# Two routing stages take over the first token turn and the first weight chunk of the expert stage behind them, and TensorE multiplies constants in them

## The reference

```
def first_block(...):            # after the mixer
    u = layer_norm(x) * (1.0 + sc_f) + sh_f
    ffn = hierarchical_moe(u, w_grp, b_grp, w_exp, b_exp, w_e_gate, w_e_up, w_e_down)
    x = layer_norm(DEEPNORM_ALPHA * x + (1.0 + gt_f) * ffn, ln2_g, ln2_b)

def moe_ffn(h, w_router, b_router, w_gu, b_gu, w_dn, b_dn):      # second block
    logits = (h @ w_router + b_router).astype(jnp.float32)
    top_logits, top_e = lax.top_k(logits, TOP_K)
    top_w = jax.nn.softmax(top_logits, axis=-1)
    ... tokens sorted by expert, each expert's list padded to blocks of 128 ...
    gu = xe @ w_gu[e] + b_gu[e]
    act = (x_lin + 1) * (x_glu * jax.nn.sigmoid(SWIGLU_ALPHA * x_glu))
    return act @ w_dn[e] + b_dn[e]
```

## Time and profile before

| | us |
|---|---|
| median of 3 runs | 2674.14 |
| lowest, highest | 2674.13, 2677.97 |
| the profiled execution, its own time | 2678.14 |
| its span, first to last instruction | 2676.4 |

### The profile page before, as it was taken

How to read it: one execution, slowest core, us unless ns; L and a number is a source line. 1 busy time by engine, 2 the same in 40 slices (tenths; PEclk the granted TensorE clock), 3 DMA queues, 4 the chain that set the end, 5 groups by cost and what they waited for, 6 DMA issues and landing times. The chain is left out here.

```text
span 2676.4 us, 38805 instructions
## 1 busy us (share of the span) xinstructions
PE 2453.7 (92%) x11850; PEld 2003.5 (75%) x11850; DVE 2141.3 (80%) x2397; ACT 1640.8 (61%) x1930; POOL 518.1 (19%) x357
## 2 busy tenths in 40 slices
PE   7987869999979998788969999999999999999994
PEld 6845657887768886777757888888888888888883
DVE  7887757999854327786558999999999999999995
ACT  3245546777744326564236777777777777777773
POOL 1214011222200003100021222222221222222220
PEclk9988869999989998899959999999999999999997
DMA  9873238999963410201258999999999999999995
GB/s 350 284 271 122 52 120 302 357 379 383 348 208 97 142 56 1 81 15 64 81 177 312 375 379 367 369 361 368 368 371 374 363 362 364 367 368 377 371 365 171
DMA packets 258910, 711.97 MB, mean 266 GB/s; under 512 B 41379, under 2 KB 74418, under 8 KB 256594
## 3 DMA queue, kind: packets, MB, share of 16 engines
q1 hardware_dynamic: 232626, 640.70, 64.4%
q0 software_dynamic: 22240, 59.80, 8.0%
q10 hardware_dynamic: 3968, 10.49, 1.0%
HBM read 691.95 MB, written 41.49 MB: 274 GB/s over the span
## 5 line engine op out<-in xcount | busy, mean ns | idle before, releaser
L52 PE MATMUL psum_all<-sb_ring_r,sb_arena_r 128*128 128x512 f32 (+1 forms) x2352 | 908.5, 386 | 0.0
L166 DVE TENSOR_TENSOR sb_ring_r<-sb_ring,sb_hi_ring_r 128x1024 fp32r<-128x1024 f32 (+1 forms) x489 | 657.9, 1395 | 136.2 <-ACT sb_hi_ring_r L157 130.4
L157 ACT ACTIVATE sb_arena_r<-sb_ring 128x1024 fp32r<-128x1024 f32 (+1 forms) x462 | 506.9, 1152 | 161.8 <-DMA sb_ring<-in_w_gu_dram 138.9
L166 DVE TENSOR_TENSOR sb_ring_r<-sb_ring,sb_arena_r 128x1024 fp32r<-128x1024 f32 (+1 forms) x462 | 593.6, 1342 | 10.2 <-ACT sb_arena_r L157 9.6
L157 ACT ACTIVATE sb_hi_ring_r<-sb_ring 128x1024 fp32r<-128x1024 f32 (+1 forms) x489 | 554.2, 1192 | 42.8 <-DMA sb_ring<-in_w_in_dram 17.9
L52 PEld LDWEIGHTS psum_all<-sb_ring_r,sb_arena_r 128*128 128x128 f32 x2352 | 447.4, 190 | 93.2
L51 PE MATMUL psum_all<-sb_hi_ring_r,sb_arena_r 128*128 128x512 f32 (+1 forms) x1304 | 497.2, 381 | 17.2 <-DVE sb_ring_r L166 5.2
L53 PE MATMUL psum_all<-sb_hi_ring_r,sb_arena_r 128*128 128x512 f32 (+1 forms) x1304 | 493.2, 378 | 0.0
L51 PE MATMUL psum_all<-sb_arena_r 128*128 128x512 f32 x1064 | 426.9, 401 | 2.9 <-DVE sb_arena_r L2467 2.9
L53 PE MATMUL psum_all<-sb_arena_r 128*128 128x512 f32 x1080 | 427.8, 396 | 0.0
L51 PEld LDWEIGHTS psum_all<-sb_hi_ring_r,sb_arena_r 128*128 128x128 f32 x1304 | 248.1, 190 | 70.3 <-issue 10.5
(11 more groups left out here) (494 smaller groups left out, 3193.3 us busy)
## 6 DMA issues: line engine op xcount, KB each, us to landing
sb_ring<-in_w_gu_dram SPq DMA_DIRECT2D x544, 512.0 KB, 6.3
sb_ring<-in_w_dn_dram SPq DMA_DIRECT2D x272, 512.0 KB, 8.5
sb_ring<-in_w_e_gate_dram SPq DMA_DIRECT2D x36, 1024.0 KB, 7.4
sb_ring<-in_w_e_up_dram SPq DMA_DIRECT2D x36, 1024.0 KB, 7.5
sb_ring<-in_w_e_down_dram SPq DMA_DIRECT2D x36, 1024.0 KB, 7.1
sb_ring<-in_w_in_dram SPq DMA_DIRECT2D x27, 1024.0 KB, 6.1
sb_arena<-in_w_ada_dram POOLq DMA_DIRECT2D x32, 512.0 KB, 5.9
sb_ring<-in_w_mod_dram SPq DMA_DIRECT2D x16, 1024.0 KB, 8.6
```

The source lines that it names most:

```text
L52: eng.matmul(out, a[0], b[1], start=False, stop=False)
L157: act.activation(s.hi[c % len(s.hi)], s.raw[c % len(s.raw)], ACT.Copy).then_inc(s.hi_made, 1)
L166: dve.tensor_tensor(s.lo[c % len(s.lo)], s.raw[c % len(s.raw)], s.hi[c % len(s.hi)].bitcast(F32), ALU.subtract).then_inc(s.lo_made, 1)
```

## The change

- In both routings TensorE starts with three 128x512 fp32 multiplications of constants (`keep_warm`), and does two more behind the turn of item 0. Nothing reads their results.
- The turn of item 0's rows, their high and low halves, and those of chunk 0 move from `experts` to the end of `route`, on the same engines. In `experts` VectorE raises the semaphores that these steps raised.
- SyncE no longer waits in `project_and_normalise` for the store of `xn` to land; it waits at the chunks in `route`, and so does GpSimd ahead of clearing `xg`, a clearing that stood first in its program.
- SyncE starts the second half of the chunks only when GpSimd has issued the gather of item 0 (`sent`).
- First block: the group choice takes one 64-element operation in place of nine small ones; the expert number is copied by VectorE, not ScalarE; the softmax weights are worked out behind the list; ScalarE's exponential stands ahead of the context squares.
- Second block: `first_rows` 0 and 1 stand behind the list's products, not ahead of them.

```
+def keep_warm(pe, k, bank, times):
+    for _ in range(times):
+        pe.matmul(k.psum[:, bank, :], k.ident[:], k.neg_sel[:, 0:4, :].rearrange("p h n -> p (h n)"), start=True, stop=True)
...
-            sp.wait_ge(s.stored, 16 * TT)
...
+            sp.wait_ge(R.x_stored, 16 * TT)
             for c, src in enumerate(first_chunks(m, e)):
+                if c == chunks_ahead(m) // 2:
+                    sp.wait_ge(s.sent, 1)
                 sp.dma_start(raw[c].rearrange("p (a b) -> p a b", a=src.shape[1]), src).then_inc(R.ahead_landed[c], 16)
...
             pool.indirect_dma_start(xg, None, m.x, bass.IndirectOffsetOnAxis(ap=R.ids[:, 0:1].bitcast(U32), axis=0),
                                     bounds_check=T - 1, oob_is_err=False).then_inc(R.gathered, 16)
+            pool.sem_inc(s.sent, 1)
 
         @block.tensor
         def _(pe):
+            keep_warm(pe, k, 0, 3)
             pe.wait_ge(s.halves, 2)
...
+            pe.wait_ge(s.list_read, 1)
+            pe.wait_ge(R.gathered, 16)
+            for kk in range(KD):
+                ins = pe.transpose(x_banks[:, kk * P:(kk + 1) * P], xg[:, kk * P:(kk + 1) * P], k.ident[:])
+            ins.then_inc(s.x_turned, 1)
+            keep_warm(pe, k, RANKS, 2)
...
+                act.wait_ge(R.ahead_landed[0], 16)
+                act.activation(hi, raw[0], ACT.Copy).then_inc(s.w_hi, 1)
+            act.wait_ge(s.x_turned, 1)
+            act.activation(x_hi, x_banks, ACT.Copy).then_inc(s.x_hi, 1)
...
-                for t in range(TT):
-                    ins = dve.tensor_tensor(four(scores)[:, t], four(logits[:, :, G:])[:, t], sel[:, t], ALU.mult)
-                link(ins)
...
+                link(dve.scalar_tensor_tensor(out=by_group(scores), in0=wide(g_other.rearrange("p t g -> p (t g)"), 2, E // G),
+                                              scalar=NEG, in1=by_group(logits), op0=ALU.mult, op1=ALU.add))
...
+            if biased:
+                weigh()
             dve.wait_ge(s.ready, 1)
             dve.wait_ge(s.ranked, 1)
...
+            if not biased:
+                dve.wait_ge(s.expert_row, 1)
+                dve.tensor_copy(R.expert_i[:, 0:NI], k.psum[:, ROW, 0:NI]).then_inc(s.items, 1)
...
+            def split_first():
+
+                dve.wait_ge(s.w_hi, 1)
+                dve.tensor_tensor(lo, raw[0], hi.bitcast(F32), ALU.subtract)
+
+            def split_rows():
+
+                dve.wait_ge(s.x_hi, 1)
+                dve.tensor_tensor(x_lo, x_banks, x_hi.bitcast(F32), ALU.subtract)
...
-            turn_x(0, True)
             pe.wait_ge(s.x_lo, 1)
...
-            make_hi(act, k, ss, 0)
             make_hi(act, k, ss, 1)
-            read_x(0, 0, False)
...
-            make_lo(dve, k, ss, 0)
-            lo_x(0, 0)
+            dve.sem_inc(ss.hi_made, 1)
+            dve.sem_inc(ss.lo_made, 1)
+            dve.sem_inc(s.x_turned, 1)
+            dve.sem_inc(s.x_hi, 1)
+            dve.sem_inc(s.x_lo, 1)
```

More of the change, by code:

```diff
@@ L1799, in route @@
     RANKS, TURNED, LIST, ROW = (4, 5, 6, 7) if biased else (1, None, 3, 2)
+    X_BANKS = slice(6, 8) if biased else slice(2, 4)
     BEYOND = T if biased else top * T
@@ L1841, in route @@
         assert at[0] <= FIRST_Y_AT - ROUTE_AT
-        xg = k.arena[:, 0:D]
+        xg, x_hi, x_lo = k.arena[:, 0:D], k.arena_r[:, D:2 * D], k.arena_r[:, 3 * D:4 * D]
+        raw = pieces([k.ring[:, i, :] for i in range(SLOTS)], m.split)
+        hi, lo = pieces([k.hi_ring[:, 0, :]], m.split)[0], pieces([k.ring_lo[:, 0, :]], m.split)[0]
+        x_banks = k.psum[:, X_BANKS, :].rearrange("p b n -> p (b n)")
         block = ctx.enter_context(nc.Block())
@@ L1874, in _ @@
             ins.then_inc(s.ready, 1)
-            pool.memset(xg, 0.0)
             if biased:
@@ L1941, in _ @@
             if biased:
+                pe.wait_ge(s.bias_landed, 96)
+                pe.wait_ge(s.comb_read, TT)
+                first_rows(0)
+                first_rows(1)
                 pe.wait_ge(s.y_made, 1)
@@ L2017, in _ @@
                 link(dve.tensor_reduce(first, g_cand, AX.X, ALU.min))
[L2018 to L2029 removed]
+                link(dve.tensor_tensor(g_other, wide(below[:, 0:G], 1, TT), wide(first, 2, G), ALU.not_equal))
+                dve.tensor_tensor(g_shift, g_log, wide(g_best, 2, G), ALU.subtract).then_inc(s.gexp_in, 1)
+                by_group = lambda x: x.rearrange("p t (g e) -> p (t g) e", g=G)
+                link(dve.scalar_tensor_tensor(out=by_group(scores), in0=wide(g_other.rearrange("p t g -> p (t g)"), 2, E // G),
+                                              scalar=NEG, in1=by_group(logits), op0=ALU.mult, op1=ALU.add))
                 by_value = scores
```

79 lines of the change are left out of this document (39 added, 40 removed).

## The result

The changed kernel took 2681.67 us (median of 13 runs, 2677.43 to 2684.41), the kernel before, run beside it, 2675.68 us (13 runs, 2674.13 to 2681.05). Ratio 1.0023, 95% interval 1.0016 to 1.0030: 4 to 8 us slower. Forecast were 2673.2 us, a range of 2668.0 to 2677.5, and a chance of 0.07 for slower. It was wrong. 1.5 us of the miss are in the starting point, since the forecast began at a median of 2674.14. A second set of runs gave 1.0018 (1.0009 to 1.0027).

A forecast was written before the change was run, and what follows sets the result against it. TensorE was taken to set the pace, with DMA just keeping up. First block +1.1, second -1.3 and -0.7, summed to -0.9 us: profiled 2678.1 to 2677.2, median 2673.2 us; range 2668.0 to 2677.5.

The forecast's parts named there:

- The barrier's last arrival moves +2.9: End of the first routing: with the moved work, the last arrival at the barrier goes from 394.6 to 397.5 us.
- I take 410.0: First expert stage: item 1's gather, issued at 401.4, lands at 410.0 us, chosen between 409.5 and 410.4.
- +1.1 us: First block's total: TensorE turns item 1's rows later, at 410.1 instead of 409.42, and more slowly, costing 1.1 us.
- Half way between: First block, turn of item 1: eight transposes take a time midway between 1.03 and 1.96 us, after TensorE idles 3 us.
- The constants ... cost nothing here: First routing: two constant products (at most 1.9 us) end by 396, and three (2.8 us) fit TensorE's idle time.
- A microsecond lost is lost: Ahead of the steady expert loop: TensorE sets the pace, so each microsecond saved or lost there is kept to the end.
- -1.3 and -0.7: Second block: first product at 1396.0 against 1397.33 (-1.3 us); half 0 has 3.3 instead of 4.7 us at low clock (-0.7).
- Gather 1 gets worse, and decides both blocks: Slower rival, both expert stages: issue and landing of item 1's gather reach 13 us; +7 us, 2681 us, chance 0.06.
- The clock carries over: Rival, both half 0 starts at 2.4 GHz: with quick gather 1 -7.0 us, chance 0.14; clock alone -3.5 us, 0.22.

## Why the prediction was wrong, step by step

**First routing, right.** "The barrier's last arrival moves +2.9": the routing is 2.4 and 3.1 us longer. Half 0 forecast 2.1 us behind the last arrival: 2.0 behind the barrier. In the changed kernel the ranks ran at the full clock (L1923 in 0.59 us, 1.00 before), worth some 0.4 us. The constants took 4.3 (three) and 3.0 to 3.2 us (two), not 2.8 and 1.9. The rows of L1919 misled: each of those products uses 32 rows of the array, and in the trace they start in pairs, 0.01 us apart, where the constants' steps start 0.85 us apart. In the first block this ended beside VectorE (395.4 against 395.3); in the second the two end last.

**First expert stage, the term that failed: item 1's gather, "I take 410.0", and "+1.1 us".** I let it take 8.6 us from its issue; it took 9.8, from 3.6 us behind the barrier on. The runs account for most of it. The issue beside VectorE's low half of chunk 1 was 2.89 us, not 2.13: the Trainium skill (page GPSIMD Engine Reference, section Specifications) says that GpSimd and VectorE contend when the VectorE instruction reads two SBUF inputs, and I had priced that in a sentence and left it out of the sum. Here the trace agrees with it in four kernels (1.07 us with no subtraction beside the issue, 2.13, 2.89, 3.06), and taking it away gave back 1.4 us of landing. The other microsecond may go to SyncE's two down chunks. Before, the first was issued at 406.96, just ahead of the landing, and the second behind it; the earlier half 0 frees their slots sooner, so they went out at 402.53 and 405.31, while the gather's rows travelled. I had not asked when slots 0 and 1 come free. Holding them back gave 8.8. Against this stands that without the hold of the first chunks the landing was 8.8 too, with the down chunks as early; so the cause of this microsecond stays open. Chunks that travel beside the gather at all are worth 3.8 us of landing (9.8 to 6.0 without any).

**"Half way between" a turn at half clock and one at full clock** was 1.97, all at half clock: 0.5 us. Behind TensorE's idle 4 us the low clock came back from 408.5 to 422.1; before, only from 415.8 to 419.2. Behind half 1's start that is 5.7 against 3.4 us of half speed, 1.1 us, of which the sum had nothing (6.1 against 4.7 in the second profiles, 0.7 us).

**"The constants ... cost nothing here" failed too.** I weighed them by their own length and by the clock that they might carry over, not by what they do to the time behind the barrier. Left out, they take 2.7 us off the first block: the barrier comes 0.6 us sooner (25.73 us of routing in place of a mean of 26.34), the gather lands 0.9 us sooner and the turn is 0.9 us shorter. So most of the gather's 1.2 us and of the turn's 0.5 are there only with the constants in place; the down chunks that then go out later are the likely link, and that is argued, not shown.

**"A microsecond lost is lost"** held, but a further 0.8 us is lost evenly over the 16 items from item 0's to item 16's scatter, in every kernel with the changed program (291.6 to 291.9 us, the turn moved or not), and in none of the three profiles without it (290.8 to 290.9). The cause is open. So the first block: +1.1 forecast, some +1.2 for the gather and 0.5 for the turn, 1.1 for the clock, 0.8 in the loop: 4.7, against 4.2 measured.

**Second block, right in direction, half the size.** Forecast -1.3 and -0.7, that is -2.0; measured -1.0. The routing's last arrival came 35.8 us behind its start (1399.07 less 1363.25), where I had 34.3 (1393.4 less 1359.06): `first_rows` 2 and 3 wait for ScalarE behind 0 and 1 (1.10 us, and 4.69 for a group of 3.79), because the list no longer covers those reads, and the constants came last. Half 1's start was 5.2 to 5.4 us nearer to the barrier, since there half 0 decides and the gather is hidden, as forecast.

**Not forecast at all: +1.3 us in a stage that the diff does not touch.** One 1 MB load there landed 6.2 to 6.8 us behind its issue in the kernels with it, 5.2 to 5.6 in the five without it for which the trace has a landing; in the changed kernel TensorE then waits 0.4 us and has some 1.3 us more at the low clock in this stage. It took 68.6 us or more in all twelve profiles of kernels with the first block's turn moved and both last constants in place, and 67.4 to 67.5 in all eight others. So it goes with the program and is hardly chance; how two products of TensorE in another stage do that is not settled. It explains about 1.3 of the 3 us that leaving out the last two constants seemed to give. With it the whole sum closes: -0.9 forecast, 3.1 more in the first block, 1.0 in the second, 1.3 here, +4.5.

**The rivals.** "Gather 1 gets worse, and decides both blocks", given 0.06, names 2681 us, and 2681.67 were measured: that is luck. It asked for a landing of 13 us and the loss in both blocks; the landing was 9.8, the gather decided the first block only, as my own forecast had it, the second block gained, and the rest came from the clock, the loop and an unchanged stage. "The clock carries over" was half right for the ranks and wrong for half 0: in the first block the granted clock stood at full from 394.8 to 398.2, while TensorE was idle but for the end of the constants (395.4), and at half again 0.5 us into half 0.

## What to carry to other kernels

Before work is moved ahead of a barrier, ask what starts only behind it and is waited for last. Here that was the second item's gather, and half 1 stood some 21 us behind the barrier in both kernels; most of the 2.7 us by which the barrier came later were lost. Where the gather was hidden, the same move did no harm and gave little (second block 1316.4 us without it, 1316.1 with it). Products that nobody reads were not free because their engine was idle: with them the clock's low stretches and the landing of a gather came elsewhere. Price a transfer by what else will be in the queue and on the issuing engine at its new time, not by its old time; and look at what stands in front of the work that waits: two reads moved one chunk back won 7 us of the changed kernel and 3 of the kernel before.

## What the runs showed of the hardware

- GpSimd's issue of an indirect DMA that finds a VectorE subtraction of two SBUF operands running ends 0.91 to 0.94 us behind that subtraction (issues of 2.10 to 3.06 us); a subtraction that starts during the issue adds nothing (1.11 us with subtractions from end to end). With none running at its start it takes 1.01 to 1.08 us.
- The same gather of 128 rows landed in 9.7 to 9.8 us (9.3 in one kernel) with VectorE beside its issue, two 1 MB chunks issued beside it and two more 3 and 6 us later; in 8.8 without the two later ones, and once in 8.8 with them; in 7.4 without VectorE either; and in 6.0 with VectorE and no chunks.
- An unchanged stage took 68.6 to 69.5 us in twelve profiles and 67.4 to 67.5 in eight, parted by the program around it. Two other unchanged stages took 203.8 and 17.3 us in one profile of the kernel before and 202.7 and 15.6 in the other.
